# A mixture-of-experts stage with wider weight chunks and rows fetched by index

## What is computed

```python
logits = einsum('bld,de->ble', h, router_w) + router_b
top_v, top_i = lax.top_k(logits, 2)
gates = sum(one_hot(top_i, 8) * softmax(top_v)[..., None], axis=-2)
for e in range(8):
    out = out + gates[..., e:e+1] * swiglu(h, wg[e], wu[e], wd[e])
```

## Time and profile before

| | us |
|---|---|
| median of three runs | 1451.0 (1450.89 to 1451.71) |
| span of the profiled execution | 1453.4 |
| TensorE busy | 1380.2 (95%) |
| VectorE busy | 1041.2 (72%) |
| ScalarE busy | 792.8 (55%) |
| DMA queue of the weights | 68.6% of 16 engines' span |
| mixture, from its first gather to the last down product | 610.1 to 1431.3 |

### The profile page before, as it was taken

How to read it: one execution, slowest core, us unless ns; L and a number is a source line. 1 busy time by engine, 2 the same in 40 slices (tenths; PEclk the granted TensorE clock), 3 DMA queues, 4 the chain that set the end, 5 groups by cost and what they waited for, 6 DMA issues and landing times.

```text
span 1453.4 us, 17788 instructions
## 1 busy us (share of the span) xinstructions
PE 1380.2 (95%) x6492; PEld 1152.1 (79%) x6493; DVE 1041.2 (72%) x1196; ACT 792.8 (55%) x892; POOL 69.2 (5%) x120
## 2 busy tenths in 40 slices
PE   5999899999998989689999999999999999999994
PEld 5986788888887977578888888888888888888883
DVE  4795633333327795568799798898887997997984
ACT  5554322232215553367677677665776766766752
POOL 1050100000000231000000000000000000000000
PEclk9999999999998999799999999999999999999997
DMA  9114433433143114379999999999999999999971
GB/s 314 67 53 159 159 116 119 141 117 117 51 150 98 47 52 124 111 261 366 332 344 358 326 348 363 312 342 367 328 347 321 348 353 324 354 355 323 346 261 70
DMA packets 252825, 343.13 MB, mean 236 GB/s; under 512 B 6252, under 2 KB 222724, under 8 KB 252758
## 3 DMA queue, kind: packets, MB, share of 16 engines
q1 hardware_dynamic: 249542, 335.78, 68.6%
q0 software_dynamic: 1424, 4.31, 1.0%
q10 hardware_dynamic: 1792, 2.18, 0.4%
HBM read 339.01 MB, written 3.23 MB: 235 GB/s over the span
## 4 chain that ended last, share of the span: by engine, by line
PE 85%; DVE 10%; ACT 2%; issue 1%; DMA 1%; POOL 0%; SPq 0%; DVEq 0%; POOLq 0%; ACTq 0%
PE ps L284 26%; PE ps L286 25%; PE ps L285 25%; DVE ps L818 5%; PE ps L1173 3%; PE ps L1120 2%; DVE w_lo L264 1%; DMA raw<-in_w_in 1%; PE ps L1184 1%; PE ps L1186 1%; PE ps L1288 1%; DVE ext L778 1%; ACT ext L504 1%; DVE x L900 1%; DVE a_lo L785 1%
## 5 line engine op out<-in xcount | busy, mean ns | idle before, releaser
L264 DVE TENSOR_TENSOR w_lo<-raw,w_hi 128x2048 fp32r<-128x2048 f32 x317 | 717.2, 2288 | 126.9 <-ACT w_hi L260 126.7
L260 ACT ACTIVATE w_hi<-raw 128x2048 fp32r<-128x2048 f32 x317 | 596.3, 1916 | 4.9 <-DMA raw<-in_w_in 4.1
L284 PE MATMUL ps<-w_hi,a_hi 128*128 128x512 f32 x1064 | 419.8, 395 | 8.2 <-DVE ft_lo L838 5.5
L286 PE MATMUL ps<-w_hi,a_lo 128*128 128x512 f32 x1064 | 415.7, 391 | 0.0
L285 PE MATMUL ps<-w_lo,a_hi 128*128 128x512 f32 x1064 | 415.7, 391 | 0.0
L543 ACT ACTIVATE ft_hi<-ps 128x256 fp32r<-128x256 f32 x121 | 46.5, 385 | 390.5 <-PE ps L1120 390.5
L284 PEld LDWEIGHTS ps<-w_hi,a_hi 128*128 128x128 f32 x1064 | 200.6, 189 | 54.3 <-issue 8.4
L286 PEld LDWEIGHTS ps<-w_hi,a_lo 128*128 128x128 f32 x1064 | 200.5, 188 | 42.0
L285 PEld LDWEIGHTS ps<-w_lo,a_hi 128*128 128x128 f32 x1064 | 200.7, 189 | 41.3 <-issue 0.6
L284 PE MATMUL ps<-w_hi,ft_hi 128*128 128x512 f32 x484 | 200.9, 415 | 0.0
L286 PE MATMUL ps<-w_hi,ft_lo 128*128 128x512 f32 x484 | 191.5, 396 | 0.0
(11 more groups left out here) (151 smaller groups left out, 957.7 us busy)
## 6 DMA issues: line engine op xcount, KB each, us to landing
raw<-in_moe_w_gate SPq DMA_DIRECT2D x88, 1024.0 KB, 7.5
raw<-in_moe_w_up SPq DMA_DIRECT2D x88, 1024.0 KB, 8.3
raw<-in_moe_w_down SPq DMA_DIRECT2D x88, 1024.0 KB, 7.5
raw<-in_w_in SPq DMA_DIRECT2D x12, 1024.0 KB, 12.0
raw<-in_dense_w_gate SPq DMA_DIRECT2D x11, 1024.0 KB, 5.4
raw<-in_dense_w_up SPq DMA_DIRECT2D x11, 1024.0 KB, 5.4
raw<-in_dense_w_down SPq DMA_DIRECT2D x11, 1024.0 KB, 5.0
raw<-in_w_out SPq DMA_DIRECT2D x8, 1024.0 KB, 5.1
```

The lines of the kernel that those rows point to most:

```text
L260: act.activation(slot(w_hi, s), slot(raw, s), ACT.Copy).then_inc(hi_ready[s], 1)
L264: dve.tensor_tensor(slot(w_lo, s), slot(raw, s), slot(w_hi, s).bitcast(F32), ALU.subtract)\
L284: pe.matmul(out, lh, rh, start=start, stop=False)
L286: return pe.matmul(out, ll, rh, start=False, stop=stop)
```

## The change

The mixture is written anew. An expert is now six steps instead of eleven units: five chunks of 512 hidden columns and one of 256. For a chunk of 512, gate and up are two tiles each (four row blocks of 512 columns, runs of 2 KB), into two PSUM banks, and down is two tiles as before; the last chunk has tiles as before. An expert still has 33 tiles, 264 matmuls for gate and up and 132 for down. The rows are stored to HBM once (`h_rows`). For each expert TensorE multiplies the one-hot matrix by the frame numbers (`index_of`), VectorE makes integers of them, GpSimd issues one indirect DMA of 128 rows of 4 KB into `xg`, and TensorE turns them with 8 transposes (`turn_rows`). The split rows have two buffers (`xT_hi[b]`, `xT_lo[b]`). The loops over units and pairs are gone: all eight experts are written out. Scatter uses banks 2 and 3 in steps 1 to 3.

The core of the new code, with the order of work of each engine in a step:

```diff
+SCATTER = {1: (0, 1), 2: (2, 3), 3: (4, 5)}
+            def slot(self, i):
+                return (i + 3 * self.b) % 6
+        def made_in(x, j, nxt):
+            gu = (x, j + 1) if j < HALF else (nxt, 0)
+            out = [(gu[0], i, gu[1]) for i in gu_kinds(gu[1])] if gu[0] is not None else []
+            return out + ([(x, 2, HALF)] if j == HALF else [(x, 4, j), (x, 5, j)])
...
+        def act_step(act, x, j, prev, nxt):
+            made = made_in(x, j, nxt)
+            gu, down = [t for t in made if t[0] is not x or t[2] != j], [t for t in made if t[0] is x and t[2] == j]
+            if j == 1 and prev is not None:
+                act.wait_ge(S["used"], TILES * x.n + 5)
+                act_ye(act, prev.n)
+            for t in gu[:1]:
+                act_moe_tile(act, *t)
+            act_moe_silu(act, x, j)
+            for t in gu[1:]:
+                act_moe_tile(act, *t)
+            if j == 0:
+                act.wait_ge(S["pt_turned"], x.n + 1)
+                act.activation(pt[x.b][:, :], ps[:, 4, 0:NTB * P], ACT.Copy).then_inc(S["pt_ready"], 1)
+            for t in down:
+                act_moe_tile(act, *t)
+            if j == 4 and nxt is not None:
+                act_xT(act, nxt)
+            act_moe_ft(act, x, j)
...
+            def dve_step(x, j, prev, nxt):
+                made = made_in(x, j, nxt)
+                before_mul = 1 if j == HALF else 2 if j == HALF - 1 else 3
+                if j == HALF and nxt is None:
+                    before_mul = 0
+                if j == 1 and prev is not None:
+                    dve_ye(prev.n)
+                for t in made[:before_mul]:
+                    moe_lo(*t)
+                moe_mul(x, j)
+                if j == 1 and nxt is not None:
+                    token_index(nxt)
+                for t in made[before_mul:]:
+                    moe_lo(*t)
+                if j in SCATTER and prev is not None:
+                    add_expert(prev, SCATTER[j])
+                if j == 4 and nxt is not None:
+                    dve_xT(nxt)
+                moe_ft(x, j)
+                if j == 0 and nxt is not None:
+                    dve.wait_ge(S["pt_turned"], x.n + 1)
+                    one_hot(nxt)
...
+            def pe_step(x, j, prev, nxt):
+                x.drained = prev is None
+                if j == 0:
+                    pe.wait_ge(S["xT_lo"], 2 * x.n + 2)
+                if j == HALF:
+                    moe_both(x)
+                else:
+                    for i in range(4):
+                        moe_half_tile(x, i, j)
+                if j == 0:
+                    turn_one_hot(x)
+                if j == 1 and nxt is not None:
+                    pe.wait_ge(S["pt_ready"], x.n + 1)
+                    index_of(nxt)
+                if j in SCATTER and prev is not None:
+                    if j == 1:
+                        pe.wait_ge(S["ye_lo_ready"], 2 * prev.n + 2)
+                    scatter(prev.n, prev.b, SCATTER[j])
+                if j == 4 and nxt is not None:
+                    if prev is not None:
+                        pe.wait_ge(S["x_added"], 18 + 6 * x.n)
+                    turn_rows(nxt)
+                if j > 0:
+                    moe_down(x, j - 1)
+                elif prev is not None:
+                    moe_down(prev, HALF)
+                moe_turn(x, j)
...
+            def index_of(x):
+                pe.wait_ge(S["onehot_ready"], x.n + 1)
+                for tb in range(NTB):
+                    ins = pe.matmul(ps[:, 4, 400:401], onehot[:, tb * P:(tb + 1) * P], tok[:, tb:tb + 1],
+                                    start=tb == 0, stop=tb == NTB - 1)
+                ins.then_inc(S["idx_done"], 1)
+            def turn_rows(x):
+                pe.wait_ge(S["gathered"], 16 * (x.n + 1))
+                for i in range(2):
+                    for k in range(4 * i, 4 * i + 4):
+                        ins = pe.transpose(ps[:, 2 + i, (k % 4) * P:(k % 4 + 1) * P], xg[:, k * P:(k + 1) * P],
+                                           ident[:, :])
+                    ins.then_inc(S["xg_turned"], 1)
...
+                pool.indirect_dma_start(out=xg[:, :], out_offset=None, in_=h_rows[:, :],
+                                        in_offset=bass.IndirectOffsetOnAxis(ap=idx[:, 0:1], axis=0),
+                                        bounds_check=TOK - 1, oob_is_err=False).then_inc(S["gathered"], 16)
```

More of the change, by code:

```diff
@@ L49 @@
 WIN = TOK
+PAD = 1024.0
 C_CB, C_LG, C_LB, C_PS, C_CW = 0, 8, 16, 24, 32
@@ L382, in units_loop @@
                 fn(f.at(rounds), l, 2 * rounds)
[L384 to L414, removed]
-                if first:
-                    start(p, spec(0))
-                run_pair(eng, unit, p, spec, first, more)
-                if not more:
[L419 to L423, removed]
+        def wanted(c, shift):
+            return 0 <= c + shift < NF
@@ new lines, in mixture, with pair, main @@
+        def mixture(eng, start, step, finish):
+            def pair(p, first, more, of):
+                x = [of(b) for b in range(3)]
+                if first:
+                    start(x[0])
+                for b in range(2):
+                    prev = of(b - 1) if b or not first else None
+                    nxt = x[b + 1] if more or b == 0 else None
+                    for j in range(NCH):
+                        step(x[b], j, prev, nxt)
+                if not more:
+                    finish(x[1])
+            def main(p):
+                return lambda b: Expert(2 * p + b, 2 * p + b, 0, b % 2, p + b // 2)
+            for p in range(PAIRS):
+                pair(p, p == 0, p < PAIRS - 1, main(p))
@@ L425, in body @@
             def body(done, e):
[L426 to L429, removed]
+                pair(done, True, False, lambda b: Expert(2 * done + b, e, 1 + b, b % 2, done))
             overflow(eng, body)
-        dense = Ffn(NTB, GEN_DENSE, 0, 0, 0)
+        dense = Ffn(0)
         def overflow(eng, body):
@@ L479, in _, with tile, start, step @@
                     sp_dense(sp, dense)
[L481 to L495, removed]
+            def tile(x, i, j):
+                load(sp, x.slot(i), x.uses(i, j), moe_src(x, i, j), moe_rows(i, j))
+            def start(x):
+                for i in gu_kinds(0):
+                    tile(x, i, 0)
+            def step(x, j, prev, nxt):
+                for made in made_in(x, j, nxt):
+                    tile(*made)
+            mixture(sp, start, step, lambda x: None)
         def act_square(act, n, tb):
@@ L544, in act_ft, with act_unit @@
                .then_inc(S["ft_hi_ready"], 1)
[L546 to L554, removed]
-                act_silu(act, f, l - 1)
[L556 to L564, removed]
+        def act_unit(act, f, l, shift):
+            if l > 0:
+                act_silu(act, f, l - 1)
+            for kind, c in f.tiles(l):
+                if wanted(c, shift):
@@ L565, in act_unit, with act_moe_tile, act_moe_silu @@
                     act_ffn_tile(act, f, kind, c)
-            if len(t) == 1 and before:
+            if l > 0:
                 act_ft(act, f, l - 1)
-        def act_xT(act, done, n):
-            act.wait_ge(S["gu_done"], done)
+        def act_moe_tile(act, x, i, j):
+            freed = x.freed(i, j)
+            if not isinstance(freed, int) or freed > 0:
+                act.wait_ge(S["used"], freed)
+            make_hi(act, x.slot(i), x.uses(i, j))
+        def act_moe_silu(act, x, j):
+            w = FT if j == HALF else CW
+            act.wait_ge(S["used"], x.gate_done(j))
+            c = x.chunk(j)
+            if not isinstance(c, int) or c > 0:
+                act.wait_ge(S["m_turned"], c)
+            act.activation(act_m[:, 0:w], ps[:, 6, 0:w], ACT.Silu).then_inc(S["m_silu"], 1)
@@ new lines, in moe_both, with moving @@
+            def moe_both(x):
+                s = x.slot(0)
+                for i in range(2):
+                    pe.wait_ge(lo_ready[x.slot(i)], x.uses(i, HALF) + 1)
+                out = ps[:, 6, :].rearrange("p (g n) -> p g n", g=2)
+                def moving(w, k):
+                    return w[:, s * TILE:(s + 2) * TILE].rearrange("p (g k n) -> p g k n", g=2, k=KD)[:, :, k, :]
+                for k in range(KD):
+                    ins = product(pe, out, xT_hi[x.b][:, k * P:(k + 1) * P], xT_lo[x.b][:, k * P:(k + 1) * P],
+                                  moving(w_hi, k), moving(w_lo, k), k == 0, k == KD - 1)
+                ins.then_inc(S["used"], 2)
@@ new lines, in moe_down @@
+            def moe_down(x, j, last=False):
+                pe.wait_ge(S["m_lo"], x.chunk(j) + 1)
+                for t, i in enumerate([2] if j == HALF else [4, 5]):
+                    s = x.slot(i)
+                    pe.wait_ge(lo_ready[s], x.uses(i, j) + 1)
+                    for r in range(2):
+                        o = (2 * t + r) * P
+                        for dh in range(2):
```

(24 more changed lines are left out.)

343 lines of the change are left out of this document (210 added, 133 removed).

## The result

The changed kernel takes 1461.5 us (1460.2 to 1464.3), the kernel before 1451.4 in the same rounds: a ratio of 1.0068, 95% interval 1.0055 to 1.0081. It is slower, where 1438 had been predicted. The profiled execution took 1458.0 us, against 1440.2 in the sum.

A forecast was written before the change was run, and what follows sets the result against it. TensorE's own instructions were taken to bound the kernel, with VectorE and the weight queue close behind. -27.6 + 14.0 + 1.4 + 1.9 - 2.9 = -13.2 from 1453.4 gives 1440.2, less 2.4: 1438 us, range 1424 to 1450.

The forecast's parts named there:

- the sum: All terms added for the profiled run: 1453.4 - 13.2 = 1440.2 us.
- What bounds the kernel: In the kernel before, TensorE's own instructions set the time, with VectorE and the queue of weights close behind.
- TensorE's floor: TensorE's own work per expert after the change: 97.3 us instead of 101.45, together -27.6 us.
- The wait of step 0: TensorE waits 2.0 us for `act_m`, behind VectorE's queued low tiles, in seven experts: +14.0 us.
- The formula for the k-th tile: After the queue's pause, weight tile k lands at about t = -8.5 + k s, with s = 2.73 us.
- the price of a wait: Step 0's waits entered the sum at their length, 2.0 us in seven experts, +14.0, with no slow clock behind them.
- Step 5's wait: TensorE waits 0.2 us for `ft_lo` before `moe_down(4)`, seven times: +1.4 us.
- the second rival: The weight queue becomes the bound: 1450 us at 2.93 a tile, 1464 at 3.00; chance of slower 0.11, no difference 0.04.
- the trace disagrees: Against the stated limit of about 358 GB/s for a core, the trace shows 368 GB/s over 40 us.
- Start, end, first fetch: First fetch 5 us, changing nothing (-3 to +3); start with slow first products and first `act_m` wait +1.9; end -2.9 us.
- the distance of 99.5: Period between experts: TensorE's 97.3 us plus waits of 2.2 us.

The follow-up runs named there:

- e10: e4_mul2_early plus 24 unused transposes during the first fetch, and in step 4 the hidden part's split before that of the next rows: 1421.9 us.
- e3_early: The changed kernel with three weight loads issued earlier by SyncE, ahead of the next expert's second and third tile: 1454.7 us.
- e2_warm: The changed kernel with 12 unused 512-column matmuls in front of the waiting turns of step 0, in seven experts: 1450.0 us.
- e1_mul2: The changed kernel with VectorE taking the product of step 0 after two low tiles instead of three: 1437.0 us.
- e4_mul2_early: The changed kernel with both edits, the step 0 product after two low tiles and three loads issued earlier: 1427.6 us.

## Why the prediction was wrong, point by point

**What bounds the kernel** was right: TensorE's own time, with VectorE's order and the queue close behind.

**TensorE's floor**, 97.3: measured 97.8 without any wait (e10). Of the 0.5, 0.2 is a slip: 101.45 less the saving of 27.6 / 7 = 3.9 is 97.5, and the sum used the 27.6. So the sum's term was 0.3 an expert, 2 us in all, too good. The pace of 0.227 was read over nine matmuls. The step of the changed kernel from one turn to the next, 17.84 us for 76 matmuls and 4 turns, gives (17.84 - 0.44) / 76 = 0.229. Gather out and turns in (0.87) were right; the index passes cost 0.56, not 0.7.

**The wait of step 0** was the right mechanism at the right place: 2.03 in expert 2, 2.0 in all experts of e3_early. As a term of the sum it was **mis-sized**: +14.0 became 18.9, because in five of the seven experts the third tile landed 0.8 to 1.2 us too late. The formula for the k-th tile gave t = 10.6; it landed at 11.9. The restart after the pause was not the weak step: in expert 1 the three first tiles, issued at 703.46, 706.26 and 706.67, landed 5.0, 5.0 and 7.3 us later, at t = -5.7, -2.9 and -0.1, where the formula has -5.8, -3.0 and -0.3. The fourth, issued at 707.22, took 10.7 and came at t = 3.8 instead of 2.4, and all behind it kept that lateness. The traffic of the DMA queues from the issue of the first of these tiles to the landing of the seventh (packets, MB, share of 16 engines), in expert 1 (703.46 to 726.04):

```profile
q1 hardware_dynamic: 3824, 8.13, 98.2%
q8 instruction: 1, 0.02, 0.3%
```

and in expert 2 (807.54 to 828.85):

```profile
q1 hardware_dynamic: 3589, 7.65, 98.2%
```

In expert 1 the DMA engines also fetched a block of 16 KB of the program's own instructions, 0.3% of 16 engines' 22.6 us, which is about 1.1 us of one engine. All five experts with a late tile (1, 3, 4, 5 and 6) have such a packet in that stretch, and neither of the two without (2 and 7) has one. The sizes fit (1.1 us taken, 1.3 us late), but this is a coincidence in seven experts and not a tested cause. The kernel before has such packets too (39 in all, the changed one 47), so they are not the price of the unrolled code alone; the prediction did not look at them.

**What failed outright** is the line after it: the price of a wait was taken as its length. The low clock behind it had been priced at the start and seen at the end of the kernel before, but not here. By the counts in the chain, 11, 0, 11, 8, 6, 4 and 5 matmuls of the seven experts run at 0.43 instead of 0.23: 45 x 0.2 = 9 us, and in five experts the four turns in front of them take 0.96 to 1.12 instead of 0.66: another 2. These 11 us are what e2_warm gave back (11.5), 1.9 for each of six falls; the shorter waits of e3_early lead to falls of 1.6. The Trainium skill, TensorE: Matmul & The Clock Gate, Part 1, says that the number of slow matmuls at the start of one and the same kernel differs between its runs. Here it differs within one run, 0 to 11 behind waits of 2.0 to 3.2 us.

**Step 5's wait** of 0.2 was right in the list of waits, 7 times; its removal gave 0.5 per expert.

**The queue** as the second rival decided by its mean rate, and the rate was good: 393 to 396 GB/s over 40 us, against 368 before. The limit of about 358 that the Trainium skill, DMA: Bandwidth & Descriptors, Specifications, states for a core is thus passed again. Further down, under Bandwidth, Measured, the same page of the Trainium skill makes it the share of a core while both cores of a pair stream. This kernel runs on one core, so its traces don't test that share, and the prediction's "the trace disagrees" says too much. What hurt was the order and the lateness of loads, which that rival named and bounded at about 2 us in all. In e1_mul2 they are worth 9.4 us, in the changed kernel 4.8 of waiting (18.9 against e3_early's 14.1).

**Start, end, first fetch** were right within 1 us: fetch 4.43 us in the chain (5 assumed), first product 10.4 us after the index began against 9.9 before, 9 products at 0.43, the first expert's wait for `act_m` 2.35 (3.2 computed, 3.34 before); at the end the wait for `ft_lo` is 0.93 (0.9 computed).

**Not in any step:** the mixture begins 3.9 us earlier than before (606.2 against 610.1) though the order of work ahead is kept. The profiles of the experiments spread over 4 us there (606.2 to 610.4), so the profile's own difference, +4.6, understates the mixture's, +8.5.

**The sum again:** the distance of 99.5 lacked 0.8 without any wait for `act_m` (98.3 in e4_mul2_early against 99.5 - 2.0 = 97.5), 0.2 for the slower turns behind a wait, 1.6 for the clock (9.7 us in experts 1 to 6), and 0.8 for the late tile: 102.9 of the 102.95 measured. In the total, 0.2 of each expert's 3.45 is the slip in the floor, which the sum did not make: 7 x 3.25 is 23 us. Less 3.9 ahead of the mixture and 0.9 in the first expert's wait it is 18, against 1458.0 - 1440.2 = 17.8 missed. The 3.9 are luck: they lie within the spread of that place, and without them more would have been missed.

**What stays open.** Why the clock fell after six waits of 2.0 us and not after the seventh, in the changed kernel in expert 2 and in e3_early in expert 3, isn't shown; nor is it tested that the fetch of instructions is what makes the tile late.

## What to carry to other kernels

When a step is given less work than its neighbours, list what the helper engines have queued before the one result that step waits for, and put that result ahead of work that is due later: one number changed here is worth 24 us, one instruction moved 25. Price a wait of TensorE as long as these (2 to 3 us) with the matmuls behind it at half rate, not only by its length. And take a change of several parts apart before judging it: of this one the fetch alone, well placed, gives 21 us, the wide runs nothing, and the new order of work, as it was first written, lost these 21 us and 10 more.

## What the runs showed of the hardware that wasn't expected

Filling a wait with useless matmuls made the kernel 11.5 us faster: seven waits of 1.1 us left the clock full, six of seven of 2.0 us did not. Runs of 2 KB in place of 1 KB raise the queue from 366 to 395 GB/s. Blocks of 16 KB of the program's instructions pass through the same 16 DMA engines as the weights, and in all five experts where a tile landed late one of them lay in the stretch before it. The indirect DMA of 128 rows of 4 KB takes 4.4 us to land beside an almost idle queue, 8.4 at the median of all eight, and up to 13.3 beside the saturated one.
